# Attention steps taken one by one, and two by two, on five in-order engines

## The reference, cut to what matters

```python
# 1. first layer: sliding window, ALiBi bias, a sink per head, 8 heads
sc = einsum('bnckgd,bnskd->bnkgcs', qb, kb) * A_HEAD_DIM ** -0.5 - slopes * dist
m = maximum(sc.max(-1), sink); pr = exp(sc - m)
o = einsum(pr / (pr.sum(-1) + exp(sink - m)), vb)
# 2. third layer: dense attention and neighbourhood attention with a bias per offset,
#    8 heads each, for the tokens; the same heads over the context alone
p = softmax(concatenate([q @ k.T, q @ kc.T]) * scale);  o = p @ concatenate([v, vc])
# 3. fourth layer: 16 heads whose queries and keys have 64 plain and 32 rotated columns
p = softmax(concatenate([q @ k.T, q @ kc.T]) * MLA_SCALE)
```

## Time and profile before

| | us |
|---|---|
| median of 3 runs | 2104.19 |
| profiled execution | 2103.52 |
| its span, first to last instruction | 2102.2 |
| PE busy | 2074.2 (99%) |
| DVE busy | 1551.2 (74%) |
| ACT busy | 1161.8 (55%) |
| stretch of ab, first bias or score to the output projection | 23.67 |
| stretch of f and e | 82.77 |
| stretch of m | 58.04 |

### The profile page before, as it was taken

The page is one execution under the profiler, slowest core; times in us unless marked ns, Lnnn a source line. Parts: engine busy times, 40 slices in busy tenths (PEclk is TensorE's granted clock), DMA queues, the critical chain, the costliest instruction groups (busy, mean ns, idle before and its releaser), DMA issues.

```text
span 2102.2 us, 33460 instructions
## 1 busy us (share of the span) xinstructions
PE 2074.2 (99%) x13896; PEld 1819.7 (87%) x13896; DVE 1551.2 (74%) x2345; ACT 1161.8 (55%) x1844; POOL 7.6 (0%) x14
## 2 busy tenths in 40 slices
PE   9999999999999999999999999999999999999998
PEld 7888898889888899998888887988888899788887
DVE  6887868877788776678876567665555778778887
ACT  6556665556555654565557568353333567766555
POOL 0000000000000000000000000000000000000000
PEclk9999999999999999999999999999999999999999
DMA  8665445665566422256652211234444544214441
GB/s 338 242 270 213 161 177 222 257 245 180 230 249 253 168 102 82 94 217 244 257 220 101 85 57 41 103 118 160 160 160 160 183 158 162 99 41 181 180 187 75
DMA packets 51271, 359.09 MB, mean 171 GB/s; under 512 B 5680, under 2 KB 5808, under 8 KB 8496
## 3 DMA queue, kind: packets, MB, share of 16 engines
q1 hardware_dynamic: 49680, 351.30, 44.2%
q10 hardware_dynamic: 1440, 5.65, 0.7%
HBM read 355.88 MB, written 1.05 MB: 170 GB/s over the span
## 4 chain that ended last, share of the span: by engine, by line
PE 81%; DVE 12%; ACT 5%; issue 1%; DMA 0%; SPq 0%; ACTq 0%; DVEq 0%
PE ps L1055 13%; PE ps L1060 7%; PE ps L3072 5%; PE ps L3073 5%; PE ps L3074 5%; DVE wl L404 4%; PE ps L1144 4%; PE ps L1145 4%; PE ps L1146 3%; PE ps L465 2%; PE ps L1382 2%; PE ps L467 2%; PE ps L466 2%; PE ps L1397 2%; PE ps L2735 2%; PE ps L2737 2%
## 5 line engine op out<-in xcount | busy, mean ns | idle before, releaser
L404 DVE TENSOR_TENSOR wl<-ring,wh 128x1024 fp32r<-128x1024 f32 x380 | 447.6, 1220 | 45.4 <-ACT wh L398 45.1
L398 ACT ACTIVATE wh<-ring 128x1024 fp32r<-128x1024 f32 x380 | 378.6, 1048 | 27.7 <-PE ps L485 9.7
L1055 PE MATMUL ps<-xs,wh 128*128 128x512 f32 x1520 | 360.0, 389 | 0.0
L1055 PEld LDWEIGHTS ps<-xs,wh 128*128 128x128 f32 x1520 | 285.3, 188 | 59.2
L1060 PEld LDWEIGHTS ps<-xs,wl 128*128 128x128 f32 x1520 | 194.9, 191 | 7.4
L1060 PE MATMUL ps<-xs,wl 128*128 128x256 f32 x1520 | 197.1, 283 | 0.0
L1144 PE MATMUL ps<-wh,hh 128*128 128x512 f32 x440 | 173.6, 395 | 1.4 <-DVE hl L1278 1.4
L1145 PE MATMUL ps<-wl,hh 128*128 128x512 f32 x440 | 172.4, 392 | 0.0
L1146 PE MATMUL ps<-wh,hl 128*128 128x512 f32 x440 | 171.3, 389 | 0.0
L3072 PE MATMUL ps<-xc,fwh 128*128 128x512 f32 (+1 forms) x384 | 143.2, 373 | 1.4 <-DVE xc L762 1.2
L3073 PE MATMUL ps<-xc,fwl 128*128 128x512 f32 (+1 forms) x384 | 142.6, 371 | 0.0
(11 more groups left out here) (588 smaller groups left out, 4638.4 us busy)
## 6 DMA issues: line engine op xcount, KB each, us to landing
ring<-wstream SPq DMA_DIRECT2D x331, 1024.0 KB, 4.9
cond_ctx<-crow ACTq DMA_DIRECT2D x3, 512.0 KB, 10.6
CN<-consts ACTq DMA_DIRECT2D x1, 1056.0 KB, 9.0
X<-xin SPq DMA_DIRECT2D x4, 256.0 KB, 5.4
ring<-wstream SPq DMA_DIRECT2D x4, 256.0 KB, 6.0
ring<-wstream SPq DMA_DIRECT2D x2, 512.0 KB, 8.3
X<-cin ACTq DMA_DIRECT2D x1, 1024.0 KB, 9.7
out<-X SPq DMA_DIRECT2D x4, 256.0 KB, 2.9
```

Source lines behind the costliest of these rows:

```text
L398: act.activation(parts_of(i)[0], gated_buffer(i) if gated(i) else tile_of(i), ACT.Copy).then_inc(high_part, tiles_done)
L404: dve.tensor_tensor(lo, w, hi.bitcast(F32), ALU.subtract).then_inc(low_part, tiles_done)
L1055: pe.matmul(ps[:, halves_bank(t) + k, :], wh[:, BUF[i0 + 3 * t + k], c, :], x[:, c, :, :].rearrange("p a n -> p (a n)"), start=(c == 0), s ...
```

## The change

The three loops now advance by two. PE's turn i holds the biases of steps i and i + 1 (now a function of its own, `ab_bias` and `e_bias`), the scores of both, the transposes of step i - 2, the values of steps i - 4 and i - 3, and the transposes of step i - 1. DVE's turn holds, for k = i and i + 1, the maximum of k and the normalisation of k - 1, then both output copies, then the work beside of both. ACT's turn holds, for k = i and i + 1, the exponentials of k, the copies of k - 2 and the work beside of k. The waits of each station stay what they were; the values are called one turn later, and in m the wait for the last copied value projections moves from turn 3 to a call of its own ahead of the first values.

```diff
+            def biases(i):
+                A, at = steps[i]
+                if i >= 2:
+                    pe.wait_ge(exped, base + i - 1)
+                if "bias" in A:
+                    A["bias"](at, step_banks(i))
...
-            for i in range(n + 3):
+            for i in range(0, n + 3, 2):
                 if i in beside:
                     beside[i]()
                 if i < n:
...
+                    biases(i)
+                    if i + 1 in beside:
+                        beside[i + 1]()
+                    biases(i + 1)
+                    scores(i)
+                    scores(i + 1)
+                if 0 <= i - 2 < n:
+                    transposes(i - 2)
+                if i == 4:
+                    if before_values:
+                        before_values()
+                if 0 <= i - 4 < n:
+                    values(i - 4)
+                    values(i - 3)
+                if 0 <= i - 2 < n:
+                    transposes(i - 1)
...
+            for i in range(0, n + 3, 2):          # DVE
+                for k in (i, i + 1):
+                    if k < n:
+                        maxima(k)
+                    if 0 <= k - 1 < n:
+                        normalised(k - 1)
+                for j in (i - 4, i - 3):
+                    if 0 <= j < n:
+                        outputs(j)
+                for k in (i, i + 1):
+                    if k < len(beside):
+                        beside[k]()
...
+            for i in range(0, n + 3, 2):          # ACT
+                for k in (i, i + 1):
+                    if k < n:
+                        exponentials(k)
+                    if 0 <= k - 2 < n:
+                        copies(k - 2)
+                    if k < len(beside):
+                        beside[k]()
...
-            pe_attention(att_m, beside={1: lambda: pe.wait_ge(*m_a.at("v03")), 2: last_values, 3: all_copied})
+            pe_attention(att_m, beside={1: lambda: pe.wait_ge(*m_a.at("v03")), 2: last_values},
+                         before_values=all_copied)
```

More of the change, by code:

```diff
@@ L1361, in att_steps, with pe_attention, scores, transposes @@
             return [(A, i) for A in parts for i in range(A["n"])], ATT0[parts[0]["name"]]
-        def pe_attention(*parts, beside={}):
+        def pe_attention(*parts, beside={}, before_values=None):
             steps, base = att_steps(parts)
             n = len(steps)
-            for i in range(n + 3):
+            def biases(i):
[4 more added lines that the diff above has]
+                    A["bias"](at, step_banks(i))
+            def scores(i):
+                A, at = steps[i]
+                A["scores"](at, step_banks(i)).then_inc(scored, 1)
+            def transposes(j):
+                if j >= 1:
+                    pe.wait_ge(p_copied, 2 * (base + j))
+                pe.wait_ge(normed, base + j + 1)
+                for h in range(2):
+                    for k in range(4):
+                        blk = 4 * h + k
+                        mm = pe.transpose(ps[:, 4 + h, k * P:(k + 1) * P],
+                                          steps[j][0]["pb"][j % 3][:, blk * P:(blk + 1) * P], ident)
+                    mm.then_inc(transposed, 1)
+            def values(j):
+                A, at_j = steps[j]
+                K, per = 1024 // A["G"], A["G"] // 2
+                b = 6 + j % 2
+                if j >= 2:
+                    pe.wait_ge(o_copied, base + j - 1)
+                pe.wait_ge(p_copied, 2 * (base + j + 1))
+                for hh in range(per):
+                    for k in range(K // P):
+                        for g in range(2):
+                            at = (g * per + hh) * K + k * P
+                            mm = pe.matmul(ps[64 * g:64 * g + 64, b, hh * P:(hh + 1) * P], A["v"](at_j, hh, g, k),
+                                           A["pt"][j % 2][:, at:at + P], start=(k == 0), stop=(k == K // P - 1),
+                                           skip_group_check=True)
+                mm.then_inc(valued, 1)
+            for i in range(0, n + 3, 2):
                 if i in beside:
@@ L1404, in dve_attention @@
             n = len(steps)
[L1405 to L1439, removed]
@@ new lines, in maxima @@
+            def maxima(i):
+                A, at = steps[i]
+                G, K = A["G"], 1024 // A["G"]
+                b0 = step_banks(i)[0]
+                nm, es = (att_small[:, i % 3, 4 * m:4 * m + G] for m in (0, 3))
+                dve.wait_ge(scored, base + i + 1)
+                top_ = dve.tensor_reduce(nm, ps[:, b0:b0 + 2, :].rearrange("p b (h k) -> p (b h) k", k=K), AX.X,
+                                         ALU.max, negate=True)
+                if A["sink"]:
+                    vdone(top_)
+                    vdone(dve.tensor_tensor(nm, nm, A["nsink"](at), ALU.min))
+                    top_ = dve.tensor_tensor(es, nm, A["sink"](at), ALU.add)
+                top_.then_inc(maxed, 1)
@@ new lines, in normalised @@
+            def normalised(j):
+                A = steps[j][0]
+                G, K = A["G"], 1024 // A["G"]
+                den, rd, es = (att_small[:, j % 3, 4 * m:4 * m + G] for m in (1, 2, 3))
+                dve.wait_ge(exped, base + j + 1)
+                if A["sink"]:
+                    vdone(dve.tensor_tensor(den, den, es, ALU.add))
+                vdone(dve.reciprocal(rd, den))
+                for m in range(G):
+                    pm = A["pb"][j % 3][:, m * K:(m + 1) * K]
+                    mul = dve.tensor_scalar(pm, pm, rd[:, m:m + 1], None, ALU.mult)
+                mul.then_inc(normed, 1)
@@ L1443, in act_attention @@
             n = len(steps)
[L1444 to L1470, removed]
@@ new lines, in copies, with exponentials @@
+            def copies(j):
+                if j >= 2:
+                    act.wait_ge(valued, base + j - 1)
+                for h in range(2):
+                    act.wait_ge(transposed, 2 * (base + j) + h + 1)
+                    act.activation(steps[j][0]["pt"][j % 2][:, 512 * h:512 * h + 512], ps[:, 4 + h, :],
+                                   ACT.Copy).then_inc(p_copied, 1)
+            def exponentials(i):
+                A = steps[i][0]
+                G, K = A["G"], 1024 // A["G"]
+                banks, per = step_banks(i), G // 2
+                nm, den, es = (att_small[:, i % 3, 4 * m:4 * m + G] for m in (0, 1, 3))
+                act.wait_ge(maxed, base + i + 1)
+                if i >= 3:
+                    act.wait_ge(transposed, 2 * (base + i - 2))
+                    act.wait_ge(normed, base + i - 2)
+                for m in range(G):
+                    e = act.activation(A["pb"][i % 3][:, m * K:(m + 1) * K],
+                                       ps[:, banks[m // per], (m % per) * K:(m % per + 1) * K], ACT.Exp,
+                                       bias=nm[:, m:m + 1], accum_out=den[:, m:m + 1])
+                if A["sink"]:
+                    e = act.activation(es, es, ACT.Exp)
+                e.then_inc(exped, 1)
```

54 lines of the change are left out of this document (16 added, 38 removed).

## The result

The changed kernel takes **2131.4 us** (median of four runs, 2130.6 to 2132.3) against 2103.4 for the kernel before (four runs): a ratio of 1.0133, 95% interval 1.0121 to 1.0144, slower by 28 us. The prediction was 2125, in a range of 2112 to 2134; the size is that of the rival in which the clock falls too (2132). The profiled execution has a span of 2129.3 us.

The account below looks back on a forecast made before the run. PE, busy 99% of the span, was taken to bound the kernel. Added waits of 4.0 us in ab, 8.3 in f and e and 8.7 in m, 21.0 on 2103.5, gave 2125 us, range 2112 to 2134.

Parts of the forecast that it names:

- the rival in which the clock falls too: Longer PE waits at starts of f and m and m's weight copies bring half clock: 2132 us; chance 0.10.
- The round: Waits close through PE, DVE and ACT; two steps of e0 take 6.36 us against 5.89, m 7.29 against 6.82.
- e0: Steps without bias in the f and e stretch: pair 6.36 us against 5.89, +0.47 over four rounds, +1.9.
- e1: Steps with a bias in the f and e stretch: pair 6.95 us against 7.06; with ACT's weight copies +0.6.
- The meetings: Where PE's blocks of different kind meet, pairing steps saves 0.36 us per pair in f, e0 and m.
- The weight copies in m: Two weight copies on ACT, turns 2 and 6, now stand in the loop of waits: 2 x 1.80 = 3.6 us more.
- f and e: Attention stretch: f +4.0, e0 +1.9, e1 +0.6, end +1.8 us; together 8.3 us more.
- ab: First attention: waits add 3.1 us, up to 1.7 more if the clock falls again; 4.0 taken.
- the third rival: PE's added waits also bring half clock, four stretches at 1.7 us on top: 2132 us; chance 0.10.
- its share for the clock: Part of the 4.0 us taken for ab that allows for the clock falling there again: 0.9 us.
- Where nothing was edited: Stretches outside the three attentions: no change, 0 us.
- the clock's rival: Half clock after PE's longer waits adds four stretches at 1.7 us to the forecast: 2132 us; chance 0.10.

Follow-up runs that it names:

- the first three runs: Changed kernel with one edit each: m's weight copies at turns 3 and 7, 2126.4 us; third transposed-probabilities buffer, 2127.3; even step's scores before the second wait, 2116.2.
- the third buffer: Changed kernel with three instead of two buffers for the copied transposes in f, e and m: 2127.3 us, ratio 1.0112.

## Why the prediction was right, and what it missed

- *The round.* Right in size and in form: e0 6.31 for 6.36, m 7.22 to 7.25 for 7.29, e1 6.81 to 6.82 for 6.95, f 7.14 to 7.16 for 7.24 (8.20 where the clock falls). The waits are where they were said to be, 0.31 for copies and 0.34 for exponentials, and the odd exponentials begin right behind copies. That each link is a cause, and not only a mark in the trace, the first three runs show. One sign isn't seen as it was said: the copy at 1270.80 begins 0.05 behind ACT's last row, with no wait shown. But it begins 1.49 behind the start of the even exponentials, and 1.34 with the third buffer, so the values held it up there too, by 0.15; in m the copies wait 0.97 and 0.48 us for L1400, the values.
- *The meetings.* 0.36 forecast, 0.38 measured in m where no wait hides it.
- *The weight copies in m.* 3.6 forecast, 3.7 given back by moving them.
- *f and e.* That 8.3 came for 8.3 is in part luck. By terms it was 5.0 for 4.0 in f (the clock's fall made that 1.0), 1.6 for 1.9 in e0, 0.1 for 0.6 in e1 and 1.6 for 1.8 at the end.
- *ab.* 3.1 and 0.9 for the clock; measured 5.8, of which the clock takes 3.5 - 1.7 = 1.8 by the granted clock. So the waits were mis-sized by 0.9 and the clock by as much.
- *The clock.* The step that failed is the argument against the third rival, that a window with 1.6 us of waits kept a clock of 1.00. In that window no single wait was over 0.75 us; those of after are 2 to 3 us, and the clock falls behind them at the start of f and in m, and twice as long in ab. That the clock follows from the waits is shown for f and m: f has the fall in all five traces of the two by two order that leave its wait empty and in none of the four that fill it, and m lost its fall when the first wait behind a weight copy was filled. For ab it is shown in the kernels where no later wait took the place of the filled one. The Trainium skill (TensorE: Matmul & The Clock Gate, Part 1) says that the clock is throttled by default and that activity releases it. The filled waits agree with that. Which waits bring a fall isn't settled: in m a single wait of 1.59 did in the run with the later weight copies, one of 1.59 did not in the run that put the scores first, and the one of 2.13 at 1863.72 did not.
- *What the falls cost.* With the one more between ab and f there are four falls more than before, 6.8 us by the granted clock. That 27.0 - 6.8 = 20.2 is the sum of the forecast without its share for the clock (20.1) is luck: the filled waits gave back 1.0 and 1.6 and not 1.7 each, and what is named under ab and in the next point wasn't in the sum.
- *Where nothing was edited.* Forecast 0, measured 3. Of this 0.78 and 0.65 are the first scores of f and m: the wait that "beside" holds at step 1 now stands ahead of the scores of step 0, which the walk through the order overlooked; it went in the run that put the scores first. The second fall between ab and f is open. The kernel of before with matmuls in its waits has two falls there as well, and its stretch between ab and f is 957.0 against 955.5, so the order of the attention isn't needed for it.

The weights were off: the clock's rival had a chance of 0.10, and the time is nearer to it than to the forecast. Its 2132 is in part luck too: the four falls that came aren't the four that it named (behind the second weight copy in m none came, and one more came in ab and one between ab and f), they cost less than 1.7 each, and the first scores and the waits of ab make up for it.

## What to carry to other kernels

Putting two steps side by side saves the engine that is full its changes of work, but it makes the next pair wait for the end of this one; walk the new loop once around through all engines, and price what each in-order queue has between the two ends. A wait added ahead of a pair should stand ahead of the half that needs it, and everything else on that queue (weight copies, waits for inputs) behind the instruction that the round waits for. Where the longest wait of PE grows, add the clock to the sum: here the falls in f and m made 2.6 us of the loss, by what the filled waits gave back.

## What the runs showed of the hardware

- Work that nobody needs, put into PE's waits, made two stretches shorter (1.0 and 1.6 us) because the clock stayed at 2.4 GHz and didn't fall to 1.2. In ab it moved the fall behind the next wait instead.
- The length of a single wait didn't tell whether the clock falls. It fell behind 1.76 us in ab and behind 1.59 in m (later weight copies). It didn't behind 2.13 in m (1863.72 in after), and not behind 1.6 in m once the 2.14 that follows was filled.
- An identity matmul of 128x128 in f32 takes 0.234 us of PE, shown as two rows of 0.117.
- The same kernel differs by 6 us between its runs with the granted clock (0.992 to 0.996).
